# Gate and up rows of two k's in one transfer, down rows in three pieces per half

## The reference

```python
gate = x_e @ w_gate_2[e]            # 32 x 1024 times 1024 x 2816
up = x_e @ w_up_2[e]                # 1024 x 2816
y = (silu(gate) * up) @ w_down_2[e] # 2816 x 1024
```

## Time and profile before

| what | value |
| --- | --- |
| time, median of 3 runs | 2227.76 us (2225.88 to 2227.81) |
| span of the profiled execution | 2223.2 us |
| median of the runs over that span | 4.6 us |
| PE busy | 1756.5 us (79%) |
| DVE busy | 638.4 us (29%) |
| ACT busy | 312.7 us (14%) |
| POOL busy | 255.8 us (12%) |
| read from HBM | 691.72 MB, 313 GB/s over the span |
| L1326, gate and up matmuls | 467.8 us busy, idle before them 283.7 us |
| L1345, down matmuls | 227.9 us busy, idle before them 113.5 us |

### The profile page before, as it was taken

How to read it: one execution, slowest core, us unless ns; L and a number is a source line. 1 busy time by engine, 2 the same in 40 slices (tenths; PEclk the granted TensorE clock), 3 DMA queues, 4 the chain that set the end, 5 groups by cost and what they waited for, 6 DMA issues and landing times.

```text
span 2223.2 us, 31988 instructions
## 1 busy us (share of the span) xinstructions
PE 1756.5 (79%) x13226; PEld 978.4 (44%) x13226; DVE 638.4 (29%) x1532; ACT 312.7 (14%) x742; POOL 255.8 (12%) x222
## 2 busy tenths in 40 slices
PE   8999999999999999986566666666665666666666
PEld 7867994886799477432121121121121122122122
DVE  3445777544477734411010010010010010010101
ACT  2241220324122013300000000000000000000001
POOL 0013880001388000000000000000000000000000
PEclk9999999999999999997777777887777876887788
DMA  8234652723554283699999999999999999999998
GB/s 293 77 114 133 213 186 95 251 77 114 169 183 153 94 315 125 248 391 424 424 424 425 425 424 425 425 424 425 426 424 425 425 424 425 425 425 425 424 426 338
DMA packets 148115, 694.00 MB, mean 312 GB/s; under 512 B 12604, under 2 KB 62588, under 8 KB 94910
## 3 DMA queue, kind: packets, MB, share of 16 engines
q1 hardware_dynamic: 144482, 683.68, 76.5%
q0 software_dynamic: 1856, 5.87, 0.8%
q10 hardware_dynamic: 1692, 3.28, 0.4%
HBM read 691.72 MB, written 4.22 MB: 313 GB/s over the span
## 4 chain that ended last, share of the span: by engine, by line
PE 52%; DMA 38%; SPq 4%; DVE 3%; issue 2%; ACT 1%; DVEq 0%; ACTq 0%
DMA arena<-in_w_up 35%; PE bank L1111 11%; PE bank L1326 7%; PE bank L711 6%; PE bank L844 6%; PE bank L1345 5%; PE bank L685 4%; SPq L437 3%; DMA arena<-in_w_down 3%; PE bank L839 1%; PE bank L1170 1%; PE bank L1051 1%; PE bank L1174 1%; PE bank L1071 1%; DVE arena L2219 1%
## 5 line engine op out<-in xcount | busy, mean ns | idle before, releaser
L1326 PE MATMUL bank<-arena 128*32 128x512 f32 (+1 forms) x3072 | 467.8, 765 | 283.7 <-DMA arena<-in_w_up 251.4
L1326 PEld LDWEIGHTS bank<-arena 128*32 128x32 f32 x3072 | 111.9, 137 | 629.1 <-DMA arena<-in_w_up 333.0
L1345 PE MATMUL bank<-arena 128*32 128x256 f32 x2816 | 227.9, 476 | 113.5 <-DMA arena<-in_w_down 105.0
L2219 DVE TENSOR_TENSOR arena<-arena,bank 64x256 f32<-64x256 f32 x96 | 40.1, 418 | 709.3 <-ACT arena L1627 707.7
L1111 PE MATMUL bank<-arena 128*128 128x128 f32 x2128 | 238.0, 274 | 0.0
L1111 PEld LDWEIGHTS bank<-arena 128*128 128x128 f32 x2128 | 237.8, 192 | 0.0
L1345 PEld LDWEIGHTS bank<-arena 128*32 128x32 f32 x2816 | 97.2, 133 | 238.7 <-DMA arena<-in_w_down 133.2
L844 PE MATMUL bank<-arena 128*128 128x256 f32 x576 | 138.6, 387 | 0.0
L711 PE MATMUL bank<-arena 128*128 128x512 f32 x308 | 133.3, 593 | 0.0
L1627 ACT ACTIVATE arena<-bank 64x512 f32<-64x512 f32 (+1 forms) x48 | 23.2, 549 | 751.1 <-PE bank L1326 751.1
L685 PE MATMUL bank<-arena 128*128 128x128 f32 (+1 forms) x992 | 118.5, 282 | 4.1 <-DMA arena<-in_w_in 2.7
(11 more groups left out here) (319 smaller groups left out, 1533.6 us busy)
## 6 DMA issues: line engine op xcount, KB each, us to landing
arena<-in_w_gate SPq DMA_DIRECT2D x127, 1408.0 KB, 20.9
arena<-in_w_up SPq DMA_DIRECT2D x127, 1408.0 KB, 23.9
arena<-in_w_down SPq DMA_DIRECT2D x144, 1024.0 KB, 17.6
arena<-in_w_down SPq DMA_DIRECT2D x32, 1536.0 KB, 13.4
arena<-in_w_up SPq DMA_DIRECT2D x44, 1024.0 KB, 7.6
arena<-in_w_in SPq DMA_DIRECT2D x40, 1024.0 KB, 8.7
arena<-in_w_out SPq DMA_DIRECT2D x12, 1024.0 KB, 6.1
arena<-in_w_down SPq DMA_DIRECT2D x12, 512.0 KB, 4.1
```

Of the source, the lines that this page charges most:

```text
L1326: last = mm(ps[b][32 * q:32 * q + 32, 0:n], expert_x[:, k, :], w, start=(k == 0), stop=(k == KT - 1))
L1345: last = mm(ps[5][32 * q:32 * q + 32, 0:256], hidden_t[:, c0 // P + r, 32 * half:32 * half + 32], down_ring[b][:, r, 256 * q:256 * q + 256 ...
L2219: last = w.tensor_mul(hidden[64 * odd:64 * odd + 64, 2 * b:2 * b + m, :], blocks(expert_gate[0:64, c0:c0 + n]), blocks(ps[b][64:P, 0:n]))
```

## The change

The host now lays gate and up out in one array `gate_up`: for expert, pair of k's and partition, the 2816 gate and 2816 up values of the first k and then those of the second, 45,056 bytes in a row. Down rows stay where they are.

* One transfer brings a pair of k's (L440 in the new numbering), 5.77 MB, into one of two pair slots. They take the place of the four slots of one k. Pair q goes to slot (q + 1) mod 2, so pair 2 goes where pair 0 was, and SP waits until both its k's are used.
* A half of the down rows is three pieces with r = 4, 4, 3, in three slots. Their rows are 16,384 and 12,288 bytes. The second one of the first expert (`SPLIT`) is fetched in two transfers of two rows each.
* PE waits once per pair. Two `keep_clock_on_rows` instead of one stand ahead of each of the last two pieces of the second half; there were three single ones before, ahead of the last three of five.
* The first expert takes its k's in the order 4, 0, 1, 2, 3, 5, 6, 7. k7 goes into `gate_up_extra`, which k4 leaves first, and k6 into the second slot. Behind them SP issues pair 0 of the next expert, then the second-half down pieces, and then pair 1.
* DVE's product (L2219) reads its operands with a stride of four values instead of two or three, since a down piece has another number of rows.

The diff:

```diff
--- before.py
+++ after.py
@@ -54,10 +54,12 @@
 LAST_ORDER = (1, 6, 2, 5, 3, 7, 4)
 UNITS_IN_2 = [0, 512, 1024, 1536, 2048, 2560]
 GU_RING = 4
+PAIR_SLOTS, KQ = GU_RING // 2, KT // 2
 HALF = FF // 2
 HT = HALF // P
 PIECES = [(0, 512), (512, 512), (1024, 384)]
-DOWN_CHUNKS = [(1024, 3), (0, 2), (256, 2), (512, 2), (768, 2)]
+DOWN_CHUNKS = [(0, 4), (512, 4), (1024, 3)]
+SPLIT = 1
 D_RING, DOWNS = len(DOWN_CHUNKS), 2 * len(DOWN_CHUNKS)
 UP_BANKS = (0, 1, 4)
 PAIR_BANKS = {0: (4, 5), 1: (0, 1)}
@@ -69,10 +71,9 @@
 SECOND_BANKS = (0, 1, 4, 5, 4, 5, 4, 5, 4, 5, 4, 5)
 SECOND_FILL = {**{i: range(3 * i, 3 * i + 3) for i in range(8)}, 8: (24,), 9: (25,), 10: (26, 27), 11: (28, 29), 12: (30, 31)}
 SECOND_READS = {1: 4, 2: 5, 3: 6, 5: 7, 6: 8, 7: 9, 10: 10, 12: 11}
-FIRST_ORDER = (1, 2, 0, 3, 4)
-FIRST_LAST = max(DOWNS // 2 + FIRST_ORDER.index(b) for b in range(3)) + 1
 AHEAD = 3
 EXTRA = GU_RING
+FIRST_KS = (4, 0, 1, 2, 3, 5, 6, 7)
 ROWS_BANKS = (2, 3, 6, 7)
 H2_BANKS = (0, 1, 4, 5)
 
@@ -213,8 +214,7 @@
 
         gate_up_ring = Region(ring_at, free).take(GU_RING, 2, FF)
         down_region = Region(ring_at + GU_RING * 2 * FF, free)
-        down_ring = [down_region.take(r, D) for _, r in DOWN_CHUNKS[1:] + DOWN_CHUNKS[:1]]
-        down_ring = down_ring[-1:] + down_ring[:-1]
+        down_ring = [down_region.take(r, D) for _, r in DOWN_CHUNKS]
         after_experts_ring = down_region.at
 
         def slot(u, n=None):
@@ -431,11 +431,14 @@
             sp.sem_inc(sem("gate_up_free"), GU_RING)
             sp.sem_inc(sem("down_free"), D_RING)
 
-            def gate_up(e, k, slot_, ahead=0):
-                to_ = gate_up_extra if slot_ == EXTRA else gate_up_ring[:, slot_]
-                for n, w in enumerate(("w_gate_2", "w_up_2")):
-                    sp.dma_start(to_[:, n, :], a[w][0, ahead:][bass.ds(e, 1), k * P:(k + 1) * P, :].rearrange("o p n -> (o p) n")
-                                 ).then_inc(sem(f"gu_in{slot_}"), 16)
+            def first_gate_up(k, slot_):
+                to_ = (gate_up_extra if slot_ == EXTRA else gate_up_ring[:, slot_]).rearrange("p g n -> p (g n)")
+                sp.dma_start(to_, a["gate_up"][0, k // 2, :, k % 2, :]).then_inc(sem(f"gu_in{slot_}"), 16)
+
+            def gate_up_pair(e, q, ahead=0):
+                s_ = (q + 1) % PAIR_SLOTS
+                sp.dma_start(gate_up_ring[:, 2 * s_:2 * s_ + 2].rearrange("p k g n -> p (k g n)"),
+                             a["gate_up"][ahead:][bass.ds(e, 1), q].rearrange("o p k n -> (o p) (k n)")).then_inc(sem(f"pair_in{s_}"), 16)
 
             def down(e, j, ahead=0):
 
@@ -445,44 +448,48 @@
                 sp.dma_start(down_ring[b].rearrange("p r n -> p (r n)"), a["w_down_2"][0, ahead:][bass.ds(e, 1), lo:lo + r * P, :].rearrange("o (p r) n -> (o p) (r n)", p=P)
                              ).then_inc(sem(f"d_in{b}"), 16)
 
+            def first_down_rows(r0):
+
+                c0, r = DOWN_CHUNKS[SPLIT]
+                rows_ = a["w_down_2"][0, 0, c0:c0 + r * P, :].rearrange("(p r) n -> p r n", r=r)
+                sp.dma_start(down_ring[SPLIT][:, r0:r0 + 2, :], rows_[:, r0:r0 + 2, :]).then_inc(sem(f"d_in{SPLIT}"), 16)
 
...
-            gate_up(0, 4, EXTRA)
+                lo = FF + half * HALF + c0
+                sp.dma_start(ahead_up[b, half], a["gate_up"][0, (EXTRA + 1) // 2, :, (EXTRA + 1) % 2, lo:lo + n]).then_inc(sem("gate_ahead_in"), 16)
+
+            first_gate_up(4, EXTRA)
             for i in range(2):
                 stream(DEPTH, 6 + i, rows(a["w_out_2"], 0, 4 * i, 4, 6 + i), ("projected_2", 2 * (3 + i)))
-            for k in (0, D_RING - 1):
-                down(0, k)
+            down(0, D_RING - 1)
+            first_down_rows(2)
             sp.wait_ge(sem("projected_2"), 12)
-            gate_up(0, 0, 0)
+            first_gate_up(0, 0)
             sp.wait_ge(sem("scores_biased"), at(DEPTH, "scores_biased", 2 * H))
             gate_ahead(1)
             up_ahead(0, 1)
 
             sp.wait_ge(sem("attended"), at(DEPTH, "attended", 8))
-            gate_up(0, 1, 1)
-            gate_up(0, 3, 3)
-            down(0, 1)
+            first_gate_up(1, 1)
+            first_gate_up(3, 3)
+            down(0, 0)
             sp.wait_ge(sem("rows_used"), (DEPTH + 1) * ROW_UNITS + 2)
-            gate_up(0, 2, 2)
-            for k in range(2, D_RING - 1):
-                down(0, k)
+            first_gate_up(2, 2)
+            first_down_rows(0)
             gate_ahead(0)
             up_ahead(2, 0)
             up_ahead(2, 1)
             sp.wait_ge(sem("logits"), T)
             up_ahead(0, 0)
 
-            def stream_gate_up(e, ks, ahead=0):
-                for k in ks:
-                    sp.wait_ge(sem("gate_up_free"), e * KT + (ahead * KT + k + 1))
-                    gate_up(e, k, (k + GU_RING - 1) % GU_RING, ahead)
+            def stream_gate_up(e, qs, ahead=0):
+                for q in qs:
+                    sp.wait_ge(sem("gate_up_free"), e * KT + (ahead * KT + 2 * q + 2))
+                    gate_up_pair(e, q, ahead)
 
             def stream_down(e, ks, ahead=0):
                 for k in ks:
@@ -490,29 +497,29 @@
                     down(e, k, ahead)
 
 
-            for k in range(GU_RING + 1, KT):
-                sp.wait_ge(sem("gate_up_free"), k)
-                if k > EXTRA + 1:
-                    gate_up(0, k, (k - 1) % GU_RING)
-                    continue
...
-            stream_gate_up(1, range(0, 2))
-            for i, b in enumerate(FIRST_ORDER):
-                sp.wait_ge(sem("down_free"), D_RING + i + 1)
-                down(0, D_RING + b)
-            stream_gate_up(1, range(2, KT))
-            sp.wait_ge(sem("down_free"), D_RING + FIRST_LAST)
+            sp.wait_ge(sem("gate_up_free"), GU_RING + 1)
+            first_gate_up(7, EXTRA)
+            sp.wait_ge(sem("gate_up_free"), GU_RING + 2)
...
+            sp.wait_ge(sem("gate_up_free"), GU_RING + 3)
+            first_gate_up(6, 1)
+            sp.wait_ge(sem("gate_up_free"), GU_RING + 5)
+            gate_up_pair(1, 0)
+            stream_down(0, range(D_RING, DOWNS))
+            sp.wait_ge(sem("gate_up_free"), GU_RING + 7)
+            gate_up_pair(1, 1)
+            stream_gate_up(1, range(2, KQ))
             stream_down(1, range(D_RING))
             stream_gate_up(2, range(1))
             stream_down(1, range(D_RING, DOWNS))
             with sp.Fori(1, NE - 2) as e:
-                stream_gate_up(e, range(1, KT), 1)
+                stream_gate_up(e, range(1, KQ), 1)
                 stream_down(e, range(D_RING), 1)
                 stream_gate_up(e, range(1), 2)
                 stream_down(e, range(D_RING, DOWNS), 1)
-            stream_gate_up(NE - 1, range(1, KT))
+            stream_gate_up(NE - 1, range(1, KQ))
             stream_down(NE - 1, range(DOWNS))
             for t in range(T):
                 for h in range(2):
@@ -1301,18 +1308,16 @@
                 pe.wait_ge(sem("expert_tokens"), e + 1)
                 if not first:
                     pe.wait_ge(sem("expert_added"), e * T)
-                for k in range(KT):
-                    if first and k == EXTRA:
-                        s_, weights = EXTRA, gate_up_extra
-                        pe.wait_ge(sem(f"gu_in{EXTRA}"), 32)
-                    elif first:
-                        n = k if k < EXTRA else k - 1
-                        s_, weights = n % GU_RING, gate_up_ring[:, n % GU_RING]
-                        pe.wait_ge(sem(f"gu_in{s_}"), 32 * (n // GU_RING + 1))
+                for i, k in enumerate(FIRST_KS if first else range(KT)):
+                    if first:
+                        s_ = {EXTRA + 1: 0, 6: 1, 7: EXTRA}.get(k, k)
+                        weights = gate_up_extra if s_ == EXTRA else gate_up_ring[:, s_]
+                        pe.wait_ge(sem(f"gu_in{s_}"), 32 if k > EXTRA else 16)
                     else:
-                        n = k + GU_RING - 1
-                        s_, weights = n % GU_RING, gate_up_ring[:, n % GU_RING]
-                        pe.wait_ge(sem(f"gu_in{s_}"), e * (KT // GU_RING * 32) + 32 * (n // GU_RING))
+                        s_ = (k // 2 + 1) % PAIR_SLOTS
+                        weights = gate_up_ring[:, 2 * s_ + k % 2]
+                        if k % 2 == 0:
+                            pe.wait_ge(sem(f"pair_in{s_}"), (e - 1) * 32 + 16 * (k // 4 + 1))
                     if first and k == EXTRA + 1:
                         pe.wait_ge(sem("gate_ahead_in"), 6 * 16)
                     for b, (c0, n) in enumerate(PIECES):
@@ -1323,7 +1328,7 @@
                                 w = ahead_gate[q][:, c0:c0 + n]
                             elif first and k == EXTRA + 1 and b != 1:
                                 w = ahead_up[b, q % 2]
-                            last = mm(ps[b][32 * q:32 * q + 32, 0:n], expert_x[:, k, :], w, start=(k == 0), stop=(k == KT - 1))
```

(15 more changed lines are left out.)

14 lines of the change are left out of this document (6 added, 8 removed).

## The result

The changed kernel takes 2260.97 us (median of 4 runs, 2257.56 to 2264.56), the kernel before 2227.10 (4 runs, 2225.88 to 2227.81). The ratio is 1.0151, with a 95% interval of 1.0139 to 1.0163: 34 us slower, where 23 were forecast. The profiled run took 2260.92 us and its span 2259.1, which is 35.9 more than the 2223.2 before.

What follows compares the result with a forecast made beforehand. The prediction took the streaming of expert weights by DMA as the bound, with TensorE keeping up. Its terms, -18.6 + 37.5 + 2.4 + 1.3 + 0.5 = +23.1 us, gave 2251 us, range 2226 to 2270.

Steps and rivals of the forecast that it cites:

- Long rows, -18.6: Weight stream: 128 fewer rows per engine and expert gain 1.2 us per expert, 18.6 us over 15.5 experts.
- no gain: Weight stream: long rows are cut up or move no faster, so the row gain is zero; 2270 us, chance 0.12.
- half the gain: Weight stream: each row saved is worth half of 9.4 ns; 2260 us, chance 0.08.
- The chain from the last landing to the issue: Expert passage: PE's remaining down work, then k0 and k1, put SP's issue of pair 2 at S + 13.75.
- S: Moment when PE sees the last down piece of an expert; the prediction counts its times from there.
- The gap, 15 x 2.5: Passages between experts: pair 2 is issued too late, losing 2.5 us (bounds 1.5 and 3.2) each, 37.5 us in all.
- So 2.4 us go before the stream runs again: Restart with an idle queue: a 1408 KB transfer took 5.8 us from issue to landing, against 3.39 streamed.
- The first stretch, +1.2: Start to the last pair of expert 1: terms 0.5 + 2.5 - 1.2 - 0.6 sorted there, +1.2 us.
- The last expert's gap: Last expert's second half, with no next pair before it: a gap of 2.05 us, 1.3 more than before.
- The tail behind the last down landing: End of the last expert: the work after the last down piece grows by 2.4 us.
- The faster rival: Expert passages: PE at 2.4 GHz issues at S + 10.9, hiding the late slot; 2212 us, chance 0.13.

Runs made afterwards that it cites:

- a light PE: The changed kernel with a quarter of the columns in every gate and up matmul and no clock-keeping matmuls: 2206.75 us, ratio 0.9902.
- the first two experiments: Both against the changed kernel: one k per slot and transfer, 2218.03 us; a quarter of gate and up columns multiplied, without keeping matmuls, 2206.75 us.
- the last: The changed kernel with one k per transfer in four slots and the down rows as before in five pieces: 2219.21 us, ratio 0.9962.
- k4 and k5 alone and no keeping matmuls: The changed kernel with pair 2 as two transfers of one k each, without clock-keeping matmuls: 2220.40 us, ratio 0.9970.

## Why the prediction was right in its direction and short in its size

* **Long rows, -18.6.** Right. 1.2 us per expert were forecast and 1.21 measured with a light PE. The rivals of no gain and of half the gain fall by the first two experiments and the last.
* **The chain from the last landing to the issue.** Right within 0.3 us in the passage shown: the issue came 13.95 us after S (S is 1581.29 + 8.6 here), forecast 13.75. Over the eight passages of this kind it is 12.6 to 14.3, at full clock 11.2 to 11.3. Keeping matmuls and the middle piece stand behind one another as worked out.
* **The gap, 15 x 2.5.** The place and the mechanism were right, its size was not. Against the stream alone (80.27) the fourteen periods of 83.42 lose 3.15 each. With k0 and k1 at 6.4 us or more (7 passages) the mean loss is 3.76 for 3.2 forecast, with 4.94 us (7 passages) 2.53 for 1.5. The step that failed is "So 2.4 us go before the stream runs again". It was read from a 1.4 MB transfer with 11 KB rows; with 45 KB rows and an empty queue it is 3.0 to 3.3, and short rows at the same place have 2.5. In the full-clock passages, where the issue is 2 us ahead, it is even 3.8 to 5.3 from the issue on. Fifteen times 0.65 is about 10 of the 12.8 us by which the spans differ more than forecast; by the medians, which leave out the 2 us named above, 11 are missing.
* **The first stretch, +1.2, was +4.2.** The second-half pieces of the first expert were issued at 987.03, for 986.9 forecast. Pair 1 of expert 1 is seen at 1017.68, which puts S at 1004.4, 1.9 later than the 1002.53 of the earlier trace rows, where +0.5 was taken (bounds 0 and 3). From there to the last pair are 42.9 us, 2.9 over three pairs of 13.3: the gap, 0.4 over the forecast. The rest is a slip in the sum: it books 1.8 us of row gain here, but between S and the last pair of expert 1 only six k's of gate and up are streamed, 40.5 us before and 40.0 by the pitch of pairs, so the gain is 0.5.
* **The last expert's gap.** 2.05 was forecast, 3.7 was measured: the down piece is seen at 2237.26, 22.07 after the last pair, where a full stream has 18.4. It is the same restart, once more too small. The tail behind the last down landing grew from 11.4 to 13.4 us, 2.0 where 2.4 were forecast.
* **The faster rival.** Its condition, an issue at S + 10.9, was nearly met in seven passages: 1518.00 is S + 11.2, if pair 1 seen at 1520.10 is S + 13.3. Yet that passage lost 2.9 us. Its rule that an issue 2.4 us ahead is enough has the same fault as the forecast.

One rule fits most of what was seen: the loss is about 3.1 us less the lead of the issue over the landing of the last transfer in the queue, and nothing from a lead of 3.1 on. In the passages shown it gives the loss at leads of 1.2, 1.4, 1.8, 3.3 and 4.7 us, and also at -0.6 (the first passage above: pair 1 is due at 1603.2, the issue is at 1603.84, and pair 2 is 3.9 us behind S + 26.6). Single passages with one keeping matmul stand up to 0.9 us off it. It is a fit, not a mechanism. It fails at the full-clock passages of the changed kernel, which lose 1.8 to 3.3 with a lead of 2.1 where the rule gives 1.0, at the first passage of the kernel without keeping matmuls (lead 2.0, loss 2.7), and at some passages with a lead over 3.1: one of the kernel with the five down pieces, and six of the kernel with k4 and k5 alone and no keeping matmuls.

The traces show what stands behind it. A transfer counts sixteen landings, one for the share of each DMA engine, and PE's wait ends with the last. The first engine is done with its share of pair 2 15.1 to 15.5 us after the issue in every passage of the changed kernel, with either lead, that is 1.8 to 2.2 over its 13.33. The kernels with one keeping matmul, with none, and with the five down pieces have 1.8 to 2.2 too. In the passage with the issue at 1603.84 the sixteen first rows start 1.0 to 2.2 us after it and take 2.4 us in the median, where later ones take 1.67. What is lost above these 2 us is the spread of the engines: the last comes 1.0 to 1.8 us behind the first where k0 and k1 ran partly at 1.2 GHz, and 1.8 to 3.3 us at full clock. There one engine stands alone, 1.2 to 2.7 us behind the fifteenth, where in the other passages the last is 0.1 to 0.6 behind it. After the issue at 1518.00 the first engine is done at 1533.27, the fifteenth at 1534.04 and the sixteenth at 1536.24. By the fifteenth landings the seven full-clock passages would lose 1.4 us in the mean, near the rule's 1.0, and not 2.55. So most of their excess is one engine that restarts late. Why it does so is open; no run changed it.
